# The transfers of the neighbourhood offsets issued from ScalarE's queue in a two-layer encoder kernel

## The reference

```python
row_off = key_rows - r[:, None] + NA_ROWS - 1
col_off = jnp.clip(c[None, :] - c[:, None], -(NA_COLS - 1), NA_COLS - 1) + NA_COLS - 1
bias = rpb[:, row_off[:, None, :, None], col_off[None, :, None, :]]
s = jnp.where(in_win[:, None, :], s + bias[None].astype(F32), -jnp.inf)
p = jax.nn.softmax(s.reshape(B, H, rows, GRID_W, kr * GRID_W), axis=-1)
```

## Time and profile before

| | |
|---|---|
| median of 3 runs | 1102.85 us (1095.15 to 1103.41) |
| the profiled execution | 1100.24 us, its span 1098.4 us |
| TensorE busy | 932.9 us (85%) |
| VectorE busy | 689.9 us (63%) |
| ScalarE busy | 539.0 us (49%) |
| GpSimd busy | 263.1 us (24%) |
| DMA, q1 (issued by SP) | 99382 packets, 137.34 MB, 45.9% of 16 engines |
| DMA, q10 (issued by ScalarE) | 7184 packets, 1.02 MB, 0.6% |
| mean granted TensorE clock | 0.950 |

### The profile page before, as it was taken

How to read it: one execution, slowest core, us unless ns; L and a number is a source line. 1 busy time by engine, 2 the same in 40 slices (tenths; PEclk the granted TensorE clock), 3 DMA queues, 4 the chain that set the end, 5 groups by cost and what they waited for, 6 DMA issues and landing times. The chain is left out here.

```text
span 1098.4 us, 19683 instructions
## 1 busy us (share of the span) xinstructions
PE 932.9 (85%) x7190; PEld 768.2 (70%) x7190; DVE 689.9 (63%) x1145; ACT 539.0 (49%) x1050; POOL 263.1 (24%) x268
## 2 busy tenths in 40 slices
PE   4888789889888898989858888798898889989896
PEld 3887568667766777767657876686776657767775
DVE  3876774546368666575558767654563696665763
ACT  3775445444344654545347754444443345554552
POOL 1452210322424003210024511112323240131100
PEclk9989989999999998999968999999899998999999
DMA  7544655325264343446255446464253633344553
GB/s 192 152 132 117 144 119 126 93 66 148 69 161 127 97 134 115 128 143 209 96 124 164 118 109 147 108 128 115 59 137 82 167 115 91 122 119 150 162 189 110
DMA packets 106669, 139.69 MB, mean 127 GB/s; under 512 B 30910, under 2 KB 51654, under 8 KB 106438
## 3 DMA queue, kind: packets, MB, share of 16 engines
q1 hardware_dynamic: 99382, 137.34, 45.9%
q10 hardware_dynamic: 7184, 1.02, 0.6%
HBM read 135.17 MB, written 6.82 MB: 129 GB/s over the span
## 5 line engine op out<-in xcount | busy, mean ns | idle before, releaser
L1457 DVE TENSOR_TENSOR w_low<-ring,w_high 128x512 fp32r<-128x512 f32 x464 | 342.9, 761 | 246.5 <-ACT w_high L1128 245.9
L1128 ACT ACTIVATE w_high<-ring 128x512 fp32r<-128x512 f32 x464 | 287.3, 630 | 316.1 <-PE pj L646 204.2
L644 PE MATMUL pj<-w_high,h_high 128*128 128x512 f32 x592 | 249.3, 421 | 42.1 <-DVE w_low L1457 23.0
L645 PE MATMUL pj<-w_low,h_high 128*128 128x512 f32 x592 | 240.2, 406 | 0.0
L646 PE MATMUL pj<-w_high,h_low 128*128 128x512 f32 x592 | 239.8, 405 | 0.0
L644 PEld LDWEIGHTS pj<-w_high,h_high 128*128 128x128 f32 x592 | 117.3, 198 | 75.9 <-DVE w_low L1457 38.4
L646 PEld LDWEIGHTS pj<-w_high,h_low 128*128 128x128 f32 x592 | 116.8, 197 | 26.5
L645 PEld LDWEIGHTS pj<-w_low,h_high 128*128 128x128 f32 x592 | 117.2, 198 | 23.6
L1133 ACT ACTIVATE big<-pair 128x512 f32<-128x512 f32 (+2 forms) x136 | 60.1, 480 | 21.7 <-PE pair L638 7.1
L2079 POOL TENSOR_TENSOR zbuf<-zbuf,mid 128x512 f32<-128x512 f32 x20 | 26.3, 1338 | 133.3 <-DVE mid L1883 133.3
L1978 POOL TENSOR_TENSOR big<-big,tab 128x256 f32<-128x256 f32 x40 | 33.2, 849 | 91.8 <-PE pair L821 59.8
(11 more groups left out here) (284 smaller groups left out, 1681.3 us busy)
## 6 DMA issues: line engine op xcount, KB each, us to landing
ring<-in_w_in SPq DMA_DIRECT2D x368, 256.0 KB, 3.0
ring<-in_w_branch SPq DMA_DIRECT2D x64, 256.0 KB, 3.1
ring<-in_w_out SPq DMA_DIRECT2D x32, 256.0 KB, 2.7
big<-skew SPq DMA_DIRECT2D x32, 128.0 KB, 3.9
skew<-in_na_rpb SPq DMA_DIRECT2D x16, 224.0 KB
out_x<-btm SPq DMA_DIRECT2D x12, 256.0 KB, 3.9
btm<-out_x SPq DMA_DIRECT2D x8, 256.0 KB, 4.9
tab<-in_table SPq DMA_DIRECT2D x1, 1408.0 KB, 7.6
```

Of the source, the lines that this page charges most:

```text
L644: mm(o, r32(a), r32(b), start=start, stop=False, skip_group_check=True)
L645: mm(o, r32(a), r32(b_low), start=False, stop=False, skip_group_check=True)
L1128: f(r32(w_high[:, u % PARTS]), ring[:, u % RAW], ACT.Copy).then_inc(w_rounded, 1)
L1457: tt(r32(w_low[:, u % PARTS]), ring[:, u % RAW], w_high[:, u % PARTS], ALU.subtract).then_inc(w_split, 1)
```

## The change

SP no longer issues any of the 24 transfers of a layer, and no longer waits for `uw` 3. ScalarE issues them: two spreads at the head of its part of each rows(s), ahead of the exponential; eight bias transfers (token tile 0) behind its copy in scan_o 3; eight more (token tile 1) behind the two squares of a_sum. The sizes and shapes of the transfers, the two hops and the buffers are as before.

The diff has a second part that changes names and bookkeeping only: a projection step now carries its first unit and its number of units, `UN` becomes `unit_no` and `depth`, the step "branch" becomes a projection of kind "branch", and `LEAD` (4) stands where `PARTS` (4) stood. With the sizes chosen, `SIZES = (4, 4)`, the order of the list, the units that each step splits, the order of the products on TensorE and all waits are those of before.

```diff
@@ SP
-                    def load_bias(i):
-                        t, half, slot = i // (2 * STEPS), i // STEPS % 2, i % STEPS
-                        row = (CHUNKS[0] + CHUNKS[1])[slot] - CHUNKS[t][half]
-                        if i == 0:
-                            sp.wait_ge(rpb_spread, 16 * NAH)
-                            sp.wait_ge(*filled(("uw", STEPS - 1)))
-                        src = bass.AP(skew.tensor, (row + 3) * C * P + GRID - 1, [[P - 1, C], [7 * C * P, NAH], [1, C]])
-                        sp.dma_start(bias[rows_of(half), t, :, slot * C:(slot + 1) * C], src).then_inc(bias_in[t], 16)
-                    def spread_rpb(h):
-                        table = na_rpb[layer, h]
-                        first = table.offset + 4 * RPB_C + WIN - 1 - (GRID - 1)
-                        src = bass.AP(table.tensor, first, [[RPB_C, 7], [0, C], [1, P]])
-                        sp.dma_start(skew[h], src).then_inc(rpb_spread, 16)
...
                         load_unit(unit)
-                        first = block_no[("c", (1, 1))]
-                        if unit % UN == 0 and 0 <= unit // UN - first < NAH:
-                            spread_rpb(unit // UN - first)
-                        after = unit - (UN * block_no[("o", (0, 1))] + RAW)
-                        if 0 <= after < 2 * NT * STEPS:
-                            load_bias(after)
@@ ScalarE
                     def rows(s):
+                        spread_rpb([2 * s, 2 * s + 1])
                         act.wait_ge(decay_arg, s + 1)
                         f(s_decay[s % 2], s_decay[s % 2], ACT.Exp, scale=-1.0).then_inc(decay_ready, 1)
...
+                    def spread_rpb(heads):
+                        for h in heads:
+                            table = na_rpb[layer, h]
+                            first = table.offset + 4 * RPB_C + WIN - 1 - (GRID - 1)
+                            src = bass.AP(table.tensor, first, [[RPB_C, 7], [0, C], [1, P]])
+                            act.dma_start(skew[h], src).then_inc(rpb_spread, 16)
+                    def load_bias(halves):
+                        act.wait_ge(rpb_spread, 16 * NAH)
+                        for t, half in halves:
+                            for slot in range(STEPS):
+                                row = (CHUNKS[0] + CHUNKS[1])[slot] - CHUNKS[t][half]
+                                src = bass.AP(skew.tensor, (row + 3) * C * P + GRID - 1, [[P - 1, C], [7 * C * P, NAH], [1, C]])
+                                act.dma_start(bias[rows_of(half), t, :, slot * C:(slot + 1) * C], src).then_inc(bias_in[t], 16)
                     def scan_o(s):
                         take(("o", s), us[:, s], four)
+                        if s == STEPS - 1:
+                            load_bias([(0, 0), (0, 1)])
                     def a_sum():
                         for t in range(NT):
                             act.wait_ge(y_summed, sum_no["a"] + t + 1)
                             f(o_sq["a"][t], o_sum["a"][t], ACT.Square).then_inc(squared_y, 1)
+                        load_bias([(1, 0), (1, 1)])
```

More of the change, by code:

```diff
@@ L211, in weight_plan, with depth @@
     for name, *args in stages:
[L212 to L220, removed]
-    return plan
+        if name != "proj":
+            continue
+        kind, arg, u, n = args
+        if kind == "branch":
+            col = arg[1] * WB
+        elif kind == "gate":
+            col = GATES + arg[0] * D + arg[1] * WB
+        else:
+            col = first[kind] + arg * (CW if kind == "conv" else WB)
+        plan += [(kind, arg, u + i, col) for i in range(n)]
+    return plan
+def depth(kind):
+    return {"conv": CUN, "branch": BK}.get(kind, KT)
 def build(nc, x_in, norm_g, w_in, conv_a, dn_a_log, dn_dt_bias, dn_norm_g, na_q_norm, na_k_norm, na_rpb,
@@ L520, in build @@
         plan = weight_plan(stages)
-        block_no = {(k, a): n for n, (k, a, _) in enumerate(plan)}
+        unit_no = {(k, a, u): n for n, (k, a, u, _) in enumerate(plan)}
         def r32(v):
@@ L601, in run @@
             for name, *args in stages:
[L602 to L605, removed]
+                if split and name == "proj":
+                    kind, arg, u, n = args
+                    unit = unit_no[(kind, arg, u)] + LEAD
+                    steps[name](*args, range(unit, min(unit + n, len(plan))))
                 elif name in steps:
@@ L724, in proj @@
-                    def proj(kind, arg):
+                        u = u0
+                        while u < u0 + count:
+                            n = 2 if u in (0, deep - 2) and u + 2 <= u0 + count else 1
+                            for t in range(NT):
+                                for v in range(u, u + n):
+                                    product(t, v)
+                            u += n
+                    def proj(kind, arg, u, n):
                         if kind == "conv":
-                            conv_product(arg)
+                            conv_product(arg, u, n)
@@ L733, in a_turn @@
+                        token_products(kind, arg, u, n, (y_high, y_low) if kind == "branch" else (h_high, h_low))
                     def a_turn(q):
@@ L1208, in proj @@
+                            if kind == "conv" and u0 + count == depth(kind):
+                                conv_take(arg)
+                            return
+                        for u in due[:-2]:
                             split(u)
-                        act.wait_ge(*front(kind, block))
-                        evict(kind, block, 0)
-                        for u in due[2:3]:
+                        act.wait_ge(*front(kind, arg))
+                        evict(kind, arg, 0)
+                        for u in due[-2:-1]:
@@ L1681, in residual, with proj @@
                         tt(v, v, b.t, ALU.add).then_inc(b.free, 1)
-                    def proj(kind, arg, due):
-                        if kind == "conv" or arg[1] == 0 or (kind[0] != "z" and kind != "out"):
+                    def proj(kind, arg, u0, count, due):
+                        last = u0 + count == depth(kind)
+                        if kind == "branch":
+                            for u in due:
+                                split(u)
+                            if last:
+                                merge(arg)
+                            return
+                        if not last or (kind[0] != "z" and kind != "out"):
                             for u in due:
```

180 lines of the change are left out of this document (81 added, 99 removed).

## The result

The changed kernel takes 1105.7 us in the median (1102.56 to 1112.81, 13 runs), the kernel before in the same measurement 1101.15 us (1095.15 to 1104.63, 13 runs). The ratio is 1.0057, interval 1.0033 to 1.0081: slower by 4 to 9 us, where 14 to 17 were forecast. The sign was right and the time lies in the range of 1098 to 1133, but the size of the change was set more than twice too large.

The account below looks back on a forecast made before the run. TensorE, busy 85% of the span, was taken as the bound, through its idle time. 26.2 us for bias transfers + 1.0 for exponentials - 10.6 of relief = 16.6 us on 1100.24: 1117 us, range 1098 to 1133.

Parts of the forecast that it names:

- The relief: Around the spreads: weight transfers no longer queue behind spreads on SP, gain 10.6 us; 1.0 us lost to a later exponential.
- five stalls: TensorE's long stalls around the spreads: 3.16 and 3.58 us in layer 1, 3.47, 2.04 and 2.42 us in layer 2.
- half of three stalls: Around the spreads: half of the stalls 3.58, 2.04 and 2.42 us, 4.0 us, was counted as gained.
- No relief: Rival: around the spreads, the same DMA engines still delay the weights, no gain; 1127 us, chance 0.13.
- The block on ScalarE: Two batches of eight bias issues stand ahead of the four splits of zd(0,1), which come 8.8 us late.
- first stall: TensorE ahead of block zd(0,1), waiting for the first split, held by ScalarE's issues and tile 0's mask: 9.8 us.
- bias term: Around block zd(0,1): bias transfers on ScalarE cost 11.6 us plus 1.5 us of clock, 13.1 us per layer.
- second stall: TensorE in zd(0,1): second mask follows the first at once, holding the second split; 4.1 us more.
- stalls of before that go: Around the bias transfers: old TensorE stalls of 2.09, 1.22 and 0.3 us fall away, per layer.
- half-covered rival: Splits of zd(0,1): short issues, masks fall between splits; 4.3 to 6.5 us per layer, 1101 to 1110 us, chance 0.32.
- Longer issues: Rival: each bias issue on ScalarE takes 0.93 us; 1128 us, chance 0.06.
- Faster: Rival: around the spreads all 14.7 us of stalls and 8 us of clock go; 1087 us, chance 0.07.

Follow-up runs that it names:

- e1: Changed kernel with the offset (bias) transfers back on SP, one behind each of 16 unit loads; spreads stay on ScalarE: 1095.18 us, ratio 0.9902 to before.
- e2: Changed kernel with the spreads back on SP; only the offset (bias) transfers on ScalarE, in two batches of eight: 1118.53 us, ratio 1.0118 to before.
- e10: Changed kernel with GpSimd's window mask cut to one row group of 32, the rest left out: 1092.73 us, ratio 0.9905 to before.
- e9: e1 with GpSimd's window mask cut to one row group of 32, the rest left out: 1077.16 us, ratio 0.9763 to before.
- e8: Changed kernel with each offset transfer cut in two, 32 issues per layer in place of 16, same bytes: 1125.98 us, ratio 1.0209 to before.
- e5: e3 with GpSimd's two masks moved behind d_rows 0 and 1: 1090.73 us, ratio 0.9894 to before.
- e11: Changed kernel with two offset transfers behind each of eight splits from zd(0,1) on, masks in their old place: 1091.66 us, ratio 0.9922 to before.
- e3: Changed kernel with one offset transfer behind each of 16 splits from zd(0,1) on, in place of two batches: 1102.95 us, ratio 1.0003 to before.
- e13: e1 with each spread issued twice by ScalarE, the second into a tensor that nothing reads: 1142.03 us, ratio 1.036 to before.
- e14: e11 with GpSimd's two masks moved behind d_rows 0 and 1: 1093.27 us, ratio 0.9926 to before.

## Why the prediction was right or wrong

**The relief: right.** It was put at 10.6 less 1.0 us; e1 measured 10.8 (7.3 to 14.3). The five stalls of the earlier trace rows did not go as said, though: the two behind L1230 vanished, but in the changed kernel one of 4.11 us stands at 131.70 us behind GpSimd's part of the tables (before: 2.44 us), and 2.42 us are left of the 3.58. The waits for weights fell by 24.1 us (55.7 to 31.6), the marks show 5.9 us of it as time in the profiled executions, and e1's timed runs 7 at the least. So the half of three stalls that was taken is borne out by the sum only, not stall by stall. What is borne out directly is the cause: the unit loads land in 3.4 to 4.2 us in the median where they took 5.9 and 6.5 us, and the eviction at L1230 (other line numbers there) ends no stall in the changed kernel and one of 0.95 us in e1, while in e2, with the spreads on SP, it still ends two of 2.84 and 2.67 us.

**"No relief": excluded** by e1.

**The block on ScalarE: right.** The splits start 11.1 us behind the copy of scan_o 3 (305.86 to 316.96), before it was 2.5 us (308.73 to 311.23): 8.6 us late, forecast 8.8. Without the mask the forecast's first split is done at 320.7 + 0.7 = 321.4, a stall of 7.3 us; e10 has 6.89, and 7.3 us by the marks. With the mask the first stall was put at 9.8 and is 8.96 and 8.92.

**The step that failed is the bias term** (13.1 us per layer), in the size of its parts. By layer 1 of the two timelines:

| term | forecast | measured |
|---|---|---|
| first stall | 9.8 | 8.96 |
| second stall, behind the second mask, and the clock | 4.1 + 1.5 | 0.77 + 0.48, and 2.1 (12 products in 4.8 us, at full clock 2.7) |
| diagonals and the transposes behind the splits | 1.3 | 0.67 + 1.15 |
| stalls of before that go | -2.1 - 1.5 | -2.09 - 1.24 - 0.41 - 1.22 - 0.32 - 0.56 |
| sum | 13.1 | 8.3 |

The marks say 7.6 and 9.3. In layer 2 the stalls grew by 5.5 us, and the other 3.8 us are products at a lower granted clock (0.50 between 865 and 870 us, and once more 0.73 between 875 and 880). The stalls of before that the earlier trace rows does not show, in layer 1:

```profile
324.43 0.47 PE L644 MATMUL pj<-w_high,h_high 128*128 128x512 f32 x1 [1.24 <-DVE zbuf L1676]
...
333.93 0.50 PE L644 MATMUL pj<-w_high,h_high 128*128 128x512 f32 x1 [0.41 <-DVE w_low L1457]
...
341.79 1.13 PE L994 MATMUL pair<-mid,tab 128*128 128x512 f32 x2 [0.32 <-POOL mid L2050]
...
352.07 0.50 PE L644 MATMUL mb<-w_high,h_high 128*128 128x512 f32 x1 [0.56 <-DVE zbuf L1883]
```

First, *the second stall*: the forecast let the second mask follow the first at once, so that one split gets through and TensorE has 1.4 us of work. In fact the second mask waited 0.98 us for its transfers (320.82, where the first had ended at 319.83), and two splits got through: TensorE ran 12 products before its next stall, and ran them near half clock (granted 0.57 between 320 and 325 us), which took 4.8 us (320.44 to 326.02 less the stall of 0.77). At full clock they take 2.7 us, and the stall would have been 2.8. The forecast added a stall and a dip, and they overlap: 3.3 us in place of 5.6.

Second, *what before already paid*: only 3.6 us of stalls were booked as falling away, where 5.8 us went. e9 (the old order of the offset transfers, with the spreads on ScalarE) shows that the masks cost that order some 6 us per layer in the marks (53.2 and 53.1 against 47.1 and 47.5), that is nearly all that they cost in the new one (60.8 - 54.4 = 6.4 and 62.4 - 54.8 = 7.6). The forecast had 7.9 us for the masks in the new order (9.8 - 7.3 of the first stall, 4.1 and 1.3), which is near what was measured, but against 3.6 in the old. Of the six stalls it counted 2.09, 1.22 and 0.3; the 1.24 us behind VectorE's zbuf, 0.41 and 0.56 were not looked for.

**The half-covered rival** (1101 to 1110 us, with a chance of 0.32) is where the time fell, but mostly not by its mechanism. It wanted short issues, and they took 0.66 us; a missing dip, and the granted clock fell to 0.50; 4.3 to 6.5 us per layer, and the marks show 7.6 and 9.3. Only its cheap second mask came true. That 1105.7 us lies in the stated range is owed to the range's width, since it is outside the forecast's own case of 1109 to 1125 us.

**Longer issues: excluded.** The issues took 0.66 us in the median, the forecast 0.62; e8 shows that the length does not depend on the number of pieces.

Two small slips in the working change nothing: the 14.14 us of the earlier trace rows are GpSimd's idle time ahead of the second mask, which began 18.7 us behind the first; and sixteen issues of 0.93 in place of 0.62 us are 5.0 us more, not 5.4.

**Faster** did not come, as both parts would have to end at their best; with the bias part in pairs or one by one (e5, e11) it does.

## What to carry to other kernels

Here a DMA issue on ScalarE was an instruction of 0.6 to 0.8 us in that engine's list. It runs beside the activation ahead of it and holds up the one behind it, so one issue behind an activation of 0.63 us cost nothing, and of a row of eight nearly all counted. Compare the length of the row with the time that the units lying ready keep TensorE busy. Spread in ones and twos among other instructions the sixteen cost nothing that could be told here, eight and eight cost 13 to 17 us. When a collision only changes its place, price the collision in the old place too (take it out of both kernels) before its price in the new place is booked as a loss. And when a new order removes a stall without removing its time, look at who now waits in another engine's list: in e3 it was the order on GpSimd.

## What was not expected of the hardware

An issue of 256 pieces took as long as one of 512 (0.638 and 0.657 us in the median). Spreads issued close behind one another on one queue do not keep their 0.76 us: of the 16 second ones of e13 the median took 3.42 us, the longest first one 6.24 us, and ScalarE stood 75.4 us. Weight transfers on the other queue landed after 4.6 and 3.8 us in the median meanwhile, against 4.2 and 3.7 us in e1. The row of eight offset transfers, 512 pieces each, shows no such growth (0.585 to 0.703 us). In e11, with splits between the pairs, the longest issue took 1.72 us, in e14 1.95 us; that is left open.
